# A decoder trunk on one core: the forget gates' product in four column groups, and the vectors' turn behind the modulation's last block

## The chip, the cores and the metric

One core of one Trainium2 chip runs the whole program in one launch. The time is device microseconds (us) of one execution. A kernel is run three times and more, and medians are compared. Engines are named as the profile names them: PE (TensorE, matrix multiply), PEld (its weight loads), DVE (VectorE), ACT (ScalarE), POOL (GpSimd), SP (SyncE, here only an issuer of DMAs).

## The reference, cut to what matters

Two layers of a causal decoder run over 1024 prompt tokens and 8 single-token samples (1032 columns, `NT`), model width 1024. In each layer a conditioning vector gives shifts, scales and gains (the modulation), a normed and modulated input `h` goes through one combined projection, and three mixers and a gated MLP follow. The part that the change touches is this:

```python
mod = jnp.dot(jax.nn.silu(c), ada_w) + ada_b                  # 1024 x 6144
sh1, sc1, g1, sh2, sc2, g2 = jnp.split(mod[:, None, :], 6, axis=-1)
h = rmsnorm(x, norms[0]) * (1 + sc1) + sh1
aq, ak, av, af, bq, bk, bv, bg, ca, cb = split_cols(jnp.dot(h, w_in))
logf = jax.nn.log_sigmoid((af + b_f).astype(F32))             # af: 4 columns of w_in
u = ca * jax.nn.sigmoid(cb)                                   # Conformer gate, then a conv of width 31
```

`af`, the forget gates' logits, has only 4 columns of `w_in` (one for each of 4 heads).

## The kernel before, in words

Activations lie with features on the 128 partitions and the 1032 tokens along the free axis; the model width is 8 slices `kk` of 128. The program is a chain of blocks with a barrier of all engines between them. In each block every engine has its own instruction list in the order of the code, and they meet through semaphores. For each layer the blocks are `block_modulation`, `block_project`, `block_mixer`, `block_tail`.

**Products.** `product3` makes one tile of 128 output rows in fp32r (a rounded float32 type) as three products: high weights by high input, high weights by low input, low weights by high input. Each is 3 matmuls of 260, 512 and 260 columns, so a slice `kk` is 9 matmuls and a tile 72. Weights come by DMA to `w_raw`; ACT rounds them to `w_hi`, POOL subtracts to get `w_lo`. Before a slice of the first tile, its hook `normed.on_pe` waits only until that slice of `h_hi` and `h_lo` is there.

**`block_modulation`.** Four blocks `b` of 512 modulation columns: PE multiplies the padded conditioning (32 stationary columns) in float32, on four column groups of the array, into `mp` (L333); ACT copies it to `mrow`; `turn(b)` turns it to partitions (L315); DVE adds the bias. `rows_of_vectors` turns the rows of biases, norms and conv weights (`vrow`) with four matmuls into `vp` (L322), and DVE copies these to `k.vecs` (L379) before anything in its list that uses them. DVE also sums squares (`macc`), PE sums them over partitions (`mst`, L405), and DVE makes the inverse root mean square from that in small operations, from a memset (L412) on. The instruction lists are strict: in DVE's, the copies of the vectors stand ahead of the additions of blocks 0 and 1, these ahead of the inverse root, and that ahead of blocks 2 and 3. The modulation's `ahead` loads the first two weight tiles of the projection and splits them, the forget tile at `COL_F` as one of them.

**`block_project`.** PE spreads the inverse root into `slot[0]` (L432). DVE, ACT and POOL then make `h` slice by slice. PE runs the forget tile first, a whole `product3` from the 128 columns at `COL_F`, of which only 4 are used, into `slot[1]`; its first instruction waits for slice 0 of `h`. Then it turns the conv contexts (L636), waits for ACT's copy of the 4 rows (`ft`, L706), turns these with 9 small matmuls (L643, `f_done`), and goes through the ten tiles of `tiles`. From the second of them on, every tile carries two slots of the remaining modulation (L651: 16 matmuls of 128 columns in float32, on four column groups, from `a_raw` in the memory of `k.x`) in front of slices 1 and 5. Before SP loads these it saves `k.x` to DRAM (`x_hold`) and waits for that. Each of the ten tiles waits for two counts:

```python
pe.wait_ge(lo_done, i + 2)
pe.wait_ge(free[s], i // 2 + s + 1)
```

The first two counts of `lo_done` are given by `pool.sem_inc` behind the last of POOL's operations on `h` (`normed.on_pool`), and the first count of `free[1]` by `act.sem_inc` behind the last of ACT's (`normed.on_act`). The forget tile waits for neither.

Of the kernel before, what the change touches and what calls it, by code (L numbers as in the profile page):

```python
# [22 lines left out]
P = 128  # L23
# [23 lines left out]
OFF = 252  # L47
# [6 lines left out]
for _name, _n in (("ident", 128), ("ones", 128), ("upto", 128), ("after", 128), ("mask", 128), ("pair", 128),  # L54
                  ("stack", 64), ("headsel", 2), ("sampsel", 8), ("decay", 512), ("xi", 256), ("zeta", 4), ("gchunk", 2),
                  ("gone", 2), ("pick", 9)):
    CONST[_name] = (_at, _n)
    _at += _n
# [3 lines left out]
def constants():  # L62
# [25 lines left out]
    put("pick", (r[:, None] % 32) == np.arange(9)[None, :])  # L88
    put("gone", np.exp(np.stack([log_g[2 * hh + hp] for hh in range(2)], 1)))
# [169 lines left out]
def block_modulation(k, L):  # L259
# [10 lines left out]
    with ExitStack() as ctx:  # L270
# [18 lines left out]
        ahead = Ahead(k, [w_in[:, :, COL_CA + DC:COL_CA + DC + P], w_in[:, :, COL_F:COL_F + P]])  # L289
# [19 lines left out]
        def _(pe):  # L309
# [212 lines left out]
def block_project(k, L):  # L522
# [4 lines left out]
    with ExitStack() as ctx:  # L527
# [5 lines left out]
        sig = ft = swap  # L533
# [27 lines left out]
        ring = lambda m: (m + 1) % 2  # L561
# [8 lines left out]
        def _(sp):  # L570
# [9 lines left out]
            for m, col in enumerate([COL_F] + tiles + [2 * HA * DA]):  # L580
                if m == 4:
# [6 lines left out]
                if 5 <= m < 5 + (PAIRS_LATE - 4) // 2:  # L588
                    for n in range(2 * m - 6, 2 * m - 4):
                        load_pair(n)  # L590
# [21 lines left out]
        def _(pool):  # L612
            plink = Link(pool, mod_link)
            plink(pool.memset(c_pad[:, :, :], 0.0))
# [4 lines left out]
            for m in range(2, 2 + nt):  # L619
# [7 lines left out]
        def _(pe):  # L627
# [3 lines left out]
            product3(pe, slot[1], k.w_hi[1], k.w_lo[1], k.h_hi, k.h_lo, KD, slice(0, P), normed.on_pe).then_inc(tile_done, 1)  # L631

            pe.wait_ge(side_loaded, 64)
            for half in range(2):
                for j in range(2):
                    last = pe.matmul(misc[1][:, 240 * j + 120 * half:240 * j + 120 * half + 120],  # L636
                                     crow[:, half, P * j:P * j + P], ident[0:120, 0:120], start=True, stop=True)
            last.then_inc(ctx_turned, 1)

            pe.wait_ge(free[1], 2)  # L640
            for c in range(TC):
                at = c * P if c < NC8 else NT - P
                last = pe.matmul(misc[0][:, HA * c:HA * c + HA], ft[0:HA, at:at + P], ident[0:HA, 0:HA], start=True, stop=True)  # L643
            last.then_inc(f_done, 1)
# [17 lines left out]
            def turn_tail():  # L662
                pe.wait_ge(free[1], 4)
# [31 lines left out]
        @block.scalar  # L695
        def _(act):
# [8 lines left out]
            act.wait_ge(tile_done, 1)  # L705
            act.activation(ft[0:HA, :], slot[1][0:HA, OFF:OFF + NT], ACT.Copy).then_inc(free[1], 1)  # L706
            for i in range(nt):
                if i + 2 < 2 + nt:
                    hi(i + 2)
                s = i % 2  # L710
# [9 lines left out]
                act.wait_ge(tile_done, i + 2)  # L720
                if i == 0:
                    act.wait_ge(f_done, 1)
                if i < 4:
                    if i == 2:
                        act.wait_ge(free[1], 3)
                    if i % 2 == 0:
                        act.activation(sig[:, :], res, ACT.Sigmoid).then_inc(free[0], 1)
# [7 lines left out]
                elif 4 <= i < 8:  # L735
                    j, dst = i % 2, (k.q_ret if i < 6 else k.k_ret)
                    scale = 1.0 if i < 6 else DB ** -0.5
# [3 lines left out]
                    else:  # L741
                        act.wait_ge(free[1], 4)
# [11 lines left out]
        def _(dve):  # L754
# [17 lines left out]
            for j in range(2):  # L772
                dve.wait_ge(free[0], 2 + j)
                dve.wait_ge(tile_done, 3 + 2 * j)
                dve.tensor_tensor(u[:, j, :], slot[1][:, OFF:OFF + NT], sig[:, :], ALU.mult).then_inc(free[1], 1)
                dve.wait_ge(free[1], 3 + j)
# [4 lines left out]
            for i in range(4, 8):  # L781
# [4 lines left out]
                dve.wait_ge(free[i % 2], {4: 4, 5: 5, 6: 5, 7: 6}[i])  # L786
# [1823 lines left out]
```

## Time and profile before

| | us |
|---|---|
| median of 3 runs (lowest, highest) | 2938.47 (2935.8, 2942.54) |
| the profiled execution, whole | 2943.78 |
| its span (first to last instruction) | 2941.5 |
| PE busy | 2808.8 (95%) |
| DVE busy | 1760.1 (60%) |
| ACT busy | 1190.2 (40%) |
| POOL busy | 199.9 (7%) |

A profile's busy time is a sum over stages with different limits. A timeline row gives the start, the length from the first start to the last end, the engine, line and operation, the number of records (x), and in brackets how long the engine sat idle before it and what ended that. A float32 matmul is two records, an fp32r matmul one. Times in the rows count from the start of the span. The first layer's modulation and projection lie at 27 to 234 us; the second layer's begin 1446 us later.

### The profile page before, as it was taken

The numbers are of one execution on the slowest core, as the hardware profiler recorded it, in microseconds if no ns is written. First come the engines' busy times: TensorE is split into PE (matmuls) and PEld (weight loads), VectorE is DVE, ScalarE is ACT, GpSimd is POOL, SyncE is SP. The second block draws the span as 40 slices with busy tenths as digits, with TensorE's granted clock in tenths as the row PEclk, the third lists the DMA queues.
The fourth block names the chain that finished last, engine by engine and source line by source line (L and its number), as shares of the span: only waits on it lengthen the run. The fifth ranks groups of instructions, "written<-read, shape, count | busy, mean of one in ns | idle before, by whom it ended". The sixth has DMA issues, their size and how long they took to land. (4 is left out here: it accounts for less than half of the span.)

```text
span 2941.5 us, 46421 instructions
## 1 busy us (share of the span) xinstructions
PE 2808.8 (95%) x18668; PEld 2463.5 (84%) x18668; DVE 1760.1 (60%) x2839; ACT 1190.2 (40%) x1897; POOL 199.9 (7%) x102
## 2 busy tenths in 40 slices
PE   6999999999999999999759999999999999999996
PEld 3888888778778899999738888897787888999995
DVE  4594444526776766676645743444567667666766
ACT  2241333525444444444332413345354445444442
POOL 1211110110000000000021210012000000000000
PEclk7999999999999999999869999999999999999998
DMA  5742112343333332333158311234332333323321
GB/s 218 234 130 51 52 51 73 93 139 94 93 94 93 93 94 88 94 93 94 32 183 244 89 48 51 52 86 122 120 96 86 94 99 93 96 87 94 94 87 69
DMA packets 430644, 293.56 MB, mean 100 GB/s; under 512 B 26493, under 2 KB 392613, under 8 KB 429630
## 3 DMA queue, kind: packets, MB, share of 16 engines
q1 hardware_dynamic: 426128, 288.45, 32.7%
q8 instruction: 148, 2.42, 0.3%
q10 hardware_dynamic: 4302, 2.15, 0.3%
q14 instruction: 66, 0.54, 0.1%
HBM read 267.68 MB, written 23.71 MB: 99 GB/s over the span
## 5 line engine op out<-in xcount | busy, mean ns | idle before, releaser
L1733 PE MATMUL tslot<-g_hi,w_hi 128*128 128x260 f32 (+1 forms) x2496 | 671.6, 323 | 9.8 <-DVE g_lo L2313 6.4
L1733 PE MATMUL tslot<-g_hi,w_lo 128*128 128x260 f32 (+1 forms) x2496 | 665.9, 321 | 0.0
L1733 PE MATMUL tslot<-g_lo,w_hi 128*128 128x260 f32 (+1 forms) x2496 | 663.5, 320 | 0.0
L1733 PEld LDWEIGHTS tslot<-g_hi,w_hi 128*128 128x128 f32 x2496 | 414.6, 189 | 52.6 <-issue 6.9
L1733 PEld LDWEIGHTS tslot<-g_hi,w_lo 128*128 128x128 f32 x2496 | 413.9, 189 | 38.0
L1733 PEld LDWEIGHTS tslot<-g_lo,w_hi 128*128 128x128 f32 x2496 | 414.0, 189 | 37.4
L1704 ACT ACTIVATE w_hi<-w_raw 128x1024 fp32r<-128x1024 f32 x292 | 307.1, 1052 | 331.5 <-PE tslot L2090 311.9
L1708 DVE TENSOR_TENSOR w_lo<-w_raw,w_hi 128x1024 fp32r<-128x1024 f32 x276 | 336.0, 1218 | 1.5 <-ACT w_hi L1704 1.5
L2398 DVE TENSOR_TENSOR cat<-cat,tslot 128x512 f32<-128x512 f32 (+1 forms) x320 | 220.5, 690 | 192.1 <-PE tslot L2090 190.9
L2090 PE MATMUL tslot<-f_hi,w_hi 128*128 128x260 f32 (+1 forms) x1056 | 283.2, 323 | 5.5 <-DVE w_lo L1708 3.3
L2090 PE MATMUL tslot<-f_hi,w_lo 128*128 128x260 f32 (+1 forms) x1056 | 281.8, 322 | 0.0
L2090 PE MATMUL tslot<-f_lo,w_hi 128*128 128x260 f32 (+1 forms) x1056 | 280.9, 320 | 0.0
L2361 DVE SCALAR_TENSOR_TENSOR bufs<-bufs,vecs 128x512 f32<-128x512 f32 x176 | 132.0, 750 | 229.3 <-ACT bufs L2238 229.3
L983 PE MATMUL dense<-h_hi,w_hi 128*128 128x344 f32 x672 | 228.9, 341 | 4.7 <-PEq L2554 4.7
L983 PE MATMUL dense<-h_lo,w_hi 128*128 128x344 f32 x672 | 217.2, 323 | 0.0
L983 PE MATMUL dense<-h_hi,w_lo 128*128 128x344 f32 x672 | 217.2, 323 | 0.0
L2090 PEld LDWEIGHTS tslot<-f_hi,w_hi 128*128 128x128 f32 x1056 | 175.2, 189 | 26.5 <-DVE cat L2398 5.5
L2090 PEld LDWEIGHTS tslot<-f_lo,w_hi 128*128 128x128 f32 x1056 | 175.7, 189 | 16.1
L2090 PEld LDWEIGHTS tslot<-f_hi,w_lo 128*128 128x128 f32 x1056 | 176.0, 190 | 14.7
L519 DVE SCALAR_TENSOR_TENSOR cat<-cat,vecs 128x1023 f32<-128x1023 f32 (+14 forms) x120 | 168.2, 1402 | 3.3
L2238 ACT ACTIVATE bufs<-bufs,vecs 128x520 f32<-128x520 f32 (+1 forms) x176 | 144.2, 820 | 18.3 <-ACT bufs L2230 0.4
L2230 ACT ACTIVATE bufs<-tslot 128x520 f32<-128x520 f32 (+1 forms) x176 | 105.5, 599 | 94.3 <-PE tslot L1733 91.4
(335 smaller groups left out, 3876.0 us busy)
## 6 DMA issues: line engine op xcount, KB each, us to landing
w_raw<-in_ffn_up_dram SPq DMA_DIRECT2D x176, 512.0 KB, 3.7
w_raw<-in_ffn_down_dram SPq DMA_DIRECT2D x88, 512.0 KB, 3.8
x_res<-in_ada_w_dram SPq DMA_DIRECT2D x64, 512.0 KB, 5.6
w_raw<-in_w_in_dram SPq DMA_DIRECT2D x46, 512.0 KB, 4.4
a_raw<-in_ada_w_dram SPq DMA_DIRECT2D x8, 2048.0 KB, 19.1
w_raw<-in_w_o_dram SPq DMA_DIRECT2D x32, 512.0 KB, 5.0
x_hold<-x_res SPq DMA_DIRECT2D x2, 4128.0 KB, 15.1
x_res<-x_hold SPq DMA_DIRECT2D x2, 4128.0 KB, 12.8
```

The lines of the kernel that those rows point to most:

```text
L519: return dve.scalar_tensor_tensor(acc, u[:, 0:TP - CTX + w], k.vecs[:, 1, 2 * w + j:2 * w + j + 1], acc, ALU.mult, ALU.add)
L983: last = pe.matmul(dense[p % 2][:, 0:b - a], w[:, kk, :], x[:, kk, a:b], start=(kk == 0 and first), stop=(kk == KD - 1 and w is w_lo))
L1704: act.activation(self.hi[n % 3][:, :, :], self.raw[n % 3][:, :, :], ACT.Copy).then_inc(self.hi_done, 1)
L1708: e.tensor_tensor(self.lo[n % 3][:, :, :], self.raw[n % 3][:, :, :], self.hi[n % 3][:, :, :].bitcast(F32), ALU.subtract).then_inc(self.dve ...
L1733: last = pe.matmul(out[:, at + a:at + b], w[:, kk, :], x[:, kk, t0 + a:t0 + b], start=(kk == 0 and first), stop=(kk == KD - 1 and w is w_lo))
L2090: last = pe.matmul(out[:, at + a:at + b], w, x[e][:, a:b], start=first and name == pairs[0], stop=final and name == pairs[-1])
L2230: act.activation(raw[half][:, 2:2 + w], out[:, at:at + w], ACT.Copy).then_inc(up_moved, 1)
L2238: act.activation(t_ab[half][:, 0:w], raw[half][:, 2:2 + w], ACT.Identity, scale=vec[:, 3, c:c + 1], bias=vec[:, 3, c + 2 * FT:c + 2 * FT + ...
L2361: dve.scalar_tensor_tensor(tt[:, 0:512], r[:, 1:513], tap1, tt[:, 0:512], ALU.mult, ALU.add).then_inc(conv, 1)
L2398: dve.tensor_tensor(y_m, y_m, out[:, at:at + w], ALU.add).then_inc(gathered, 1)
```

## The change

The forget gates no longer have a tile. Their 4 columns are loaded alone into a zeroed `wf_pad` of 32 columns, and after the first real tile PE multiplies them in plain float32 on four column groups (slices `kk` and `kk+4` on group `kk`), 48 matmuls into `slot[0]`. ACT copies all 128 rows to `ft` (now in `k.cat`), and the turn to tokens sums the four groups through a constant `pickf`. The tile list is one shorter; the two tiles loaded ahead are the first two real ones; slots and rings change parity. In the modulation, `rows_of_vectors` stands behind the product of block 3 in place of block 1.

```diff
-        ahead = Ahead(k, [w_in[:, :, COL_CA + DC:COL_CA + DC + P], w_in[:, :, COL_F:COL_F + P]])
+        ahead = Ahead(k, [w_in[:, :, COL_CA + DC:COL_CA + DC + P], w_in[:, :, COL_CA:COL_CA + P]])
...
-                if b == 1:
+                if b == 3:
                     rows_of_vectors()
                 if b >= 1:
                     turn(b - 1)
...
-            for m, col in enumerate([COL_F] + tiles + [2 * HA * DA]):
-                if m == 4:
+            for m, col in enumerate(tiles + [2 * HA * DA]):
+                if m == 0:
+                    sp.wait_ge(wf_zero, 1)
+                    sp.dma_start(wf_pad[:, :, 0:HA], w_in[:, :, COL_F:COL_F + HA]).then_inc(wf_loaded, 16)
+                if m == 3:
                     sp.dma_start(k.x_hold.rearrange("p (a b) -> p a b", b=NT), k.x[:, :, :]).then_inc(x_held, 16)
...
-            product3(pe, slot[1], k.w_hi[1], k.w_lo[1], k.h_hi, k.h_lo, KD, slice(0, P), normed.on_pe).then_inc(tile_done, 1)
...
+            def forget_product():
+                pe.wait_ge(wf_loaded, 16)
+                pe.wait_ge(free[0], 1)
+                for k0 in (0, 4):
+                    for x, first in ((k.h_hi, True), (k.h_lo, False)):
+                        for a, b in CHUNKS:
+                            for g in range(4):
+                                last = pe.matmul(slot[0][32 * g:32 * g + 32, OFF + a:OFF + b], wf_pad[:, k0 + g, :], x[:, k0 + g, a:b].bitcast(F32),
+                                                 start=(k0 == 0 and first), stop=(k0 == 4 and not first), skip_group_check=True)
+                last.then_inc(f_product, 1)
+
+            def forget_rows():
+                pe.wait_ge(free[0], 2)
+                for c in range(TC):
+                    at = c * P if c < NC8 else NT - P
+                    last = pe.matmul(misc[0][:, HA * c:HA * c + HA], ft[:, at:at + P], const(k, "pickf"), start=True, stop=True)
+                last.then_inc(f_done, 1)
...
+                    if i == 0:
+                        normed.on_pe(e, kk)
+                    if i == 1 and kk == 0:
+                        forget_rows()
                     if i >= 1 and kk in (1, 5):
                         mod_slot(2 * i - 2 + kk // 4)
...
             for i in range(nt):
-                s = i % 2
-                pe.wait_ge(lo_done, i + 2)
-                pe.wait_ge(free[s], i // 2 + s + 1)
-                product3(pe, slot[s], k.w_hi[s], k.w_lo[s], k.h_hi, k.h_lo, KD, slice(0, P), mod_hook(i)).then_inc(tile_done, 1)
+                s, w = slot_of(i), ring(i)
+                pe.wait_ge(lo_done, i + 1)
+                pe.wait_ge(free[s], i // 2 + (1 if s else 2))
+                product3(pe, slot[s], k.w_hi[w], k.w_lo[w], k.h_hi, k.h_lo, KD, slice(0, P), mod_hook(i)).then_inc(tile_done, 1)
+                if i == 0:
+                    forget_product()
+                    turn_contexts()
```

On PE, at the start of the first layer's projection, the order before is this. The three `pdiag` matmuls are the spread, and the first `h_hi,w_hi` is the forget tile; signal6 and signal7 count what DVE and POOL have made of `h`.

```order
L432 MATMUL slot<-pdiag,consts 128x260 [waits signal9]
L432 MATMUL slot<-pdiag,consts 128x512
L432 MATMUL slot<-pdiag,consts 128x260
L154 MATMUL slot<-h_hi,w_hi 128x260 [waits signal6,signal7]
L154 MATMUL slot<-h_hi,w_hi 128x512
```

At the same place of the changed kernel the first `h_hi,w_hi` is the tile at `COL_CA + DC`; signal24 is `free[1]` and signal26 is `lo_done`.

```order
L433 MATMUL slot<-pdiag,consts 128x260 [waits signal9]
L433 MATMUL slot<-pdiag,consts 128x512
L433 MATMUL slot<-pdiag,consts 128x260
L155 MATMUL slot<-h_hi,w_hi 128x260 [waits signal7,signal6,signal24,signal26]
L155 MATMUL slot<-h_hi,w_hi 128x512
```

The first product after the spread has two more waits. Behind that product PE's list before went on with the contexts, the 9 turns of the forget rows (`swap` is `ft`) and the first real tile.

```order
L154 MATMUL slot<-h_hi,w_lo 128x260
L636 MATMUL misc<-consts,ctxrow 128x120 [waits signal28]
L636 MATMUL misc<-consts,ctxrow 128x120 x3
L643 MATMUL misc<-consts,swap 128x4 [waits signal24]
L643 MATMUL misc<-consts,swap 128x4 x8
L154 MATMUL slot<-h_hi,w_hi 128x260 [waits signal23,signal26]
```

In the changed kernel the same stretch of PE's list reads so (`cat` is the new `ft`; signal23 is `free[0]`, signal43 `wf_loaded`).

```order
L155 MATMUL slot<-h_hi,w_lo 128x260
L655 MATMUL slot<-h_hi,wf_pad 32x260 [waits signal23,signal43]
L655 MATMUL slot<-h_hi,wf_pad 32x260 x3
L655 MATMUL slot<-h_hi,wf_pad 32x512 x4
L655 MATMUL slot<-h_hi,wf_pad 32x260 x4
L655 MATMUL slot<-h_lo,wf_pad 32x260 x4
...
L644 MATMUL misc<-consts,ctxrow 128x120 [waits signal28]
L644 MATMUL misc<-consts,ctxrow 128x120 x3
L663 MATMUL misc<-consts,cat 128x4 [waits signal23,signal26]
L663 MATMUL misc<-consts,cat 128x4 x8
L155 MATMUL slot<-h_hi,w_hi 128x260
```

The 48 matmuls stand between the first real tile and the contexts, and the forget rows are turned in front of the second real tile. In the modulation (first layer) PE's list in the changed kernel ends with the four turns of the vectors (`vp`) between the last product and the last two turns; before, they stood behind the second product.

```order
L334 MATMUL mp<-a_raw,c_pad 32x512 [waits signal3,a_early3]
L334 MATMUL mp<-a_raw,c_pad 32x512 x7
L323 MATMUL vp<-consts,vrow 128x88 [waits signal7]
L323 MATMUL vp<-consts,vrow 128x62
L323 MATMUL vp<-consts,vrow 128x88 x2
L316 MATMUL mtp<-consts,mrow 128x9 [waits signal5,signal3]
```

DVE's list is the same in both kernels, with the copies from `vp` ahead of all its additions and of the inverse root.

## Rows read from the trace of the kernel before

**Rows 1.** The page's part 1: busy time of PE, share of the span, instructions.
```profile
PE 2808.8 (95%) x18668; PEld 2463.5 (84%) x18668; DVE 1760.1 (60%) x2839; ACT 1190.2 (40%) x1897; POOL 199.9 (7%) x102
```

**Rows 2.** Timeline of PE, first layer's projection: start, length, row, [idle before <- releaser].
```profile
73.28 1.20 PE L154 MATMUL slot<-h_hi,w_hi 128*128 128x260 f32 x3 [6.94 <-POOL h_lo L468]
...
88.04 1.05 PE L636 MATMUL misc<-consts,ctxrow 120*128 120x120 f32 x8
...
91.42 1.23 PE L154 MATMUL slot<-h_hi,w_hi 128*128 128x260 f32 x3
...
104.32 0.63 PE L154 MATMUL slot<-h_hi,w_hi 128*128 128x260 f32 x3
...
105.83 1.08 PE L651 MATMUL misc<-x_res,pc_pad 128*32 128x128 f32 x32
106.84 0.74 PE L154 MATMUL slot<-h_hi,w_hi 128*128 128x260 f32 x3
```

**Rows 3.** Waits between 60 and 90 us: total, times, longest.
```profile
PE slot L154 <- POOL h_lo L468: 7.8, 3, 6.9
```

**Rows 4.** Timelines of POOL, ACT and SP in the same block.
```profile
82.65 2.42 POOL L468 TENSOR_TENSOR h_lo<-cat,h_hi 128x1024 fp32r<-128x1024 f32 x1 [1.28 <-ACT h_hi L481]
...
83.67 1.15 ACT L483 ACTIVATE h_hi<-cat,mod 128x1024 fp32r<-128x1024 f32 x1 [1.10 <-DVE cat L496]
...
82.65 1.02 SPq L593 DMA_DIRECT2D w_raw<-in_w_in_dram  x2
...
99.36 11.28 SPq L578 DMA_DIRECT2D x_res<-in_ada_w_dram  x8
```

**Rows 5.** Timelines of PE and ACT, second layer's projection.
```profile
1527.34 1.20 PE L154 MATMUL slot<-h_hi,w_hi 128*128 128x260 f32 x3 [6.94 <-POOL h_lo L468]
...
1537.73 1.15 ACT L483 ACTIVATE h_hi<-cat,mod 128x1024 fp32r<-128x1024 f32 x1 [1.10 <-DVE cat L496]
```

**Rows 6.** Windows: length, busy us (records) of each engine, PE clock, DMA.
```profile
28.20:33.30 5.10, 5.07 (x24) 1.19 (x28) 0.79 (x1) 2.84 (x3) 0.00 (x0) 0.50 1.05 407
33.30:36.00 2.70, 1.06 (x12) 0.12 (x4) 2.63 (x3) 2.70 (x4) 0.00 (x0) 1.00 1.07 395
...
91.30:94.40 3.10, 3.10 (x13) 2.81 (x13) 0.20 (x1) 1.28 (x1) 1.33 (x1) 0.50 1.13 490
```

**Rows 7.** Timeline of PE in the mixer: two float32 matmuls of 512 columns.
```profile
240.61 1.96 PE L996 MATMUL sc<-prob,consts 128*128 128x512 f32 x4
```

**Rows 8.** Timelines of PE, ACT and DVE, first layer's modulation.
```profile
41.12 2.43 PE L322 MATMUL vp<-consts,vrow 88*128 88x88 f32 x8 [6.76 <-DMA vrow<-in_ffn_conv_w_dram]
43.34 1.78 PE L315 MATMUL mtp<-consts,mrow 128*128 128x9 f32 x8
...
57.34 1.95 PE L315 MATMUL mtp<-consts,mrow 128*128 128x9 f32 x16
...
38.54 1.07 ACT L359 ACTIVATE mrow<-mp 128x512 f32<-128x512 f32 x2
...
43.66 0.69 DVE L379 COPY vecs<-vp 128x88 f32<-128x88 f32 x4 [2.32 <-PE vp L322]
...
54.11 0.07 DVE L412 MEMSET mv<- 128x9 f32 x1 [3.37 <-PE mst L405]
...
58.51 0.20 DVE L388 TENSOR_TENSOR mod<-mtp,vecs 128x36 f32<-128x36 f32 x1 [1.91 <-PE mtp L315]
...
59.56 0.23 DVE L398 SCALAR_TENSOR_TENSOR mod<-mod,vecs 128x72 f32<-128x72 f32 x1
```

**Rows 9.** Timelines of PE and DVE, second layer's modulation.
```profile
1492.87 2.37 PE L333 MATMUL mp<-a_raw,c_pad 128*32 128x512 f32 x16 [2.66 <-DMA a_raw<-in_ada_w_dram]
...
1499.11 3.64 PE L333 MATMUL mp<-a_raw,c_pad 128*32 128x512 f32 x16
...
1511.40 1.95 PE L315 MATMUL mtp<-consts,mrow 128*128 128x9 f32 x16
...
1513.63 0.23 DVE L398 SCALAR_TENSOR_TENSOR mod<-mod,vecs 128x72 f32<-128x72 f32 x1
```

More of the change, by code:

```diff
@@ L532, in block_project @@
         u = k.cat[:, 4:6, :]
-        sig = ft = swap
+        sig, ft = swap, k.cat[:, 2, :]
+        wf_pad = sb("wf_pad", [P, KD, 32])
         bf = sb("bf", [P, HA])
@@ L560, in block_project @@
         U_DONE = 3
-        ring = lambda m: (m + 1) % 2
+        ring = lambda m: m % 2
+        slot_of = lambda i: (i + 1) % 2
+        wf_zero, wf_loaded, f_product = (k.sem(n) for n in ("wf_zero", "wf_loaded", "f_product"))
         arena = k.x[:, :, :].rearrange("p a b -> p (a b)")
@@ L587, in _ @@
                         load_pair(n)
-                if 5 <= m < 5 + (PAIRS_LATE - 4) // 2:
-                    for n in range(2 * m - 6, 2 * m - 4):
+                if 4 <= m < 4 + (PAIRS_LATE - 4) // 2:
+                    for n in range(2 * m - 4, 2 * m - 2):
                         load_pair(n)
@@ L613, in _ @@
             plink = Link(pool, mod_link)
+            pool.memset(wf_pad[:, :, :], 0.0).then_inc(wf_zero, 1)
             plink(pool.memset(c_pad[:, :, :], 0.0))
@@ L618, in _ @@
             pool.sem_inc(lo_done, 1)
-            for m in range(2, 2 + nt):
+            for m in range(2, 1 + nt):
                 pool.wait_ge(hi_done, m - 1)
@@ L630, in _, with turn_contexts @@
             pe_spread(k, pe, diag, slot[0]).then_inc(rb_ready, 1)
-            product3(pe, slot[1], k.w_hi[1], k.w_lo[1], k.h_hi, k.h_lo, KD, slice(0, P), normed.on_pe).then_inc(tile_done, 1)
[L633 to L644, printed above, removed]
+            def turn_contexts():
+                pe.wait_ge(side_loaded, 64)
+                for half in range(2):
+                    for j in range(2):
+                        last = pe.matmul(misc[1][:, 240 * j + 120 * half:240 * j + 120 * half + 120],
+                                         crow[:, half, P * j:P * j + P], ident[0:120, 0:120], start=True, stop=True)
+                last.then_inc(ctx_turned, 1)
+            def forget_product():
[14 more added lines that the diff above has]
+                last.then_inc(f_done, 1)
             def mod_product(n):
@@ L662, in turn_tail @@
             def turn_tail():
-                pe.wait_ge(free[1], 4)
+                pe.wait_ge(free[0], 4)
                 for j in range(2):
@@ L703, in hi @@
                 act.activation(k.w_hi[ring(m)][:, :, :], k.w_raw[ring(m)][:, :, :], ACT.Copy).then_inc(hi_done, 1)
-            act.wait_ge(tile_done, 1)
-            act.activation(ft[0:HA, :], slot[1][0:HA, OFF:OFF + NT], ACT.Copy).then_inc(free[1], 1)
             for i in range(nt):
-                if i + 2 < 2 + nt:
-                    hi(i + 2)
-                s = i % 2
+                if i >= 1:
+                    hi(i + 1)
+                s = slot_of(i)
                 res = slot[s][:, OFF:OFF + NT]
@@ L719, in _ @@
                         act.activation(mrow[:, :], misc[1][:, 0:2 * P], ACT.Copy).then_inc(row_ready, 1)
-                act.wait_ge(tile_done, i + 2)
-                if i == 0:
-                    act.wait_ge(f_done, 1)
+                act.wait_ge(tile_done, i + 1)
                 if i < 4:
                     if i == 2:
-                        act.wait_ge(free[1], 3)
+                        act.wait_ge(free[0], 3)
                     if i % 2 == 0:
-                        act.activation(sig[:, :], res, ACT.Sigmoid).then_inc(free[0], 1)
+                        act.activation(sig[:, :], res, ACT.Sigmoid).then_inc(free[1], 1)
+                    if i == 0:
+                        act.wait_ge(f_product, 1)
+                        act.activation(ft[:, :], slot[0][:, OFF:OFF + NT], ACT.Copy).then_inc(free[0], 1)
                     if i == 3:
@@ L741, in _ @@
                     else:
-                        act.wait_ge(free[1], 4)
+                        act.wait_ge(free[0], 4)
                     for quad in range(4):
@@ L772, in _ @@
             for j in range(2):
[L773 to L776, printed above, removed]
+                dve.wait_ge(free[1], 2 + j)
+                dve.wait_ge(tile_done, 2 + 2 * j)
+                dve.tensor_tensor(u[:, j, :], slot[0][:, OFF:OFF + NT], sig[:, :], ALU.mult).then_inc(free[0], 1)
+                dve.wait_ge(free[0], 3 + j)
                 taps(*((0, 17) if j == 0 else (17, 26)))
@@ L785, in _ @@
                 dve.wait_ge(rope_raw, 3 * (i - 3))
-                dve.wait_ge(free[i % 2], {4: 4, 5: 5, 6: 5, 7: 6}[i])
+                dve.wait_ge(free[slot_of(i)], {4: 4, 5: 5, 6: 5, 7: 6}[i])
                 dve.tensor_tensor(swap[:, :], swap[:, :], rope[:, 1, :], ALU.mult).then_inc(rope_link, 1)
```

5 lines of the change are left out of this document (4 added, 1 removed).

## The prediction, as it was written before the result was known

> **What bounds the kernel now.** I read the page's busy times first: PE is busy for 95% of the span [rows 1], so an instruction taken from PE is worth its time wherever PE runs without a gap, and a gap on PE is worth its length. Next I read the timeline of PE in the first layer's projection [rows 2]. There PE is not dense at the front: it sits idle for 6.94 us until the first slice of `h` is split, starts the forget tile at 73.28 and ends it at 88.04. The waits of that stretch [rows 3] say that inside the tile only 7.8 - 6.94 = 0.86 us more are waited. The forget tile is therefore made almost wholly while DVE, ACT and POOL are still making `h`, which they end some 12 us after its start: the last operation of POOL on `h` starts at 82.65, that of ACT at 83.67 [rows 4]. From 88.04 on PE is dense. The second layer repeats it within 0.1 us [rows 5]. So the question is not only what the forget product costs, but what stands in its place under the making of `h`.
>
> **The start of the first tile.** In the changed order the first product of the block is a tile of the loop, and the loop waits for `lo_done` and `free[1]`, which the forget tile did not. Both counts are given behind the last piece of `h`, one by POOL, one by ACT. Slice-wise waits are still there, but they no longer matter, because the product cannot begin before all of `h` is nearly ready. When is such a count given? SP's weight loads wait for the same `lo_done`, and they are issued at 82.65, the very moment at which POOL's last operation starts [rows 4], not at its end, 85.07. So ACT's count comes at about 83.67 and the first tile starts then: 83.67 - 73.28 = 10.4 us later. If ACT's count comes only at the end of its operation (1.15 us), it is 11.5. What is got back is the 0.86 us of waits inside the tile. In the second layer it is 1537.73 - 1527.34 = 10.4 again [rows 5]. The half clock of a first tile, after PE's idle time, goes with it in either order. The end of the first tile moves by 10.4 - 0.9 = +9.5 us in each layer (up to +10.6).
>
> **The forget product.** It is 48 matmuls, that is 4 x 4 x 1032 = 16,512 columns, in float32 on four column groups. The trace has this kind twice. At full clock 16 matmuls of 128 columns take 106.84 - 105.83 = 1.01 us [rows 2], 0.493 ns a column, which gives 8.1 us. At half clock 24 records, 12 matmuls of 512 columns, take 5.1 us [rows 6], 0.83 ns a column or 0.415 at full clock, which gives 6.9 us. The chunks are 260 and 512 long, nearer to the second: I take 7.4 us. The clock at which it runs is full, I think: PE comes from a dense tile, and the window from 28.20 to 33.30 held just such products, and the one behind it ran at full clock [rows 6].
>
> Does the overlap of the groups hold? A full-width float32 matmul shows what four serial groups would cost: two matmuls of 512 columns in 1.96 us [rows 7], 1.91 ns a column, 3.9 times the first value. The rows therefore show nearly full overlap. The Trainium skill (TensorE: Matmul & The Clock Gate, Part 3: Packing small matmuls) is less generous: four tiles by rows measured 3.07x, three by columns 2.38x. By 3.07x the product would take 1.91 x 16,512 / 3.07 = 10.3 us in place of 7.4. The trace disagrees for 128 columns; for the chunk lengths here, only the changed kernel can say.
>
> **What goes.** One full tile per layer. The one from 91.42 to 104.32 took 12.9 us [rows 2], of which 3.1 us ran at half clock [rows 6], the fall that follows the small matmuls of contexts and forget rows. That fall stays, since the same small matmuls now stand ahead of the second real tile, so 12.9 - 1.55 = 11.35 us go. Contexts, copy and forget rows keep their 3.4 us (88.04 to 91.42): the copy is of 128 partitions in place of 4, with as many columns for each.
>
> Per layer: 9.5 + 7.4 - 11.35 = +5.55 us, and +11.1 for both (bounds +10.1 with 6.9 us, +14.7 with 8.1 and the late count). Behind it everything in the block moves with PE. SP loads one weight tile less ahead of its save of `k.x`, so the modulation's pairs come no later than now (first issue 99.36, in use at 105.83 without a gap), and PE asks for them at about 111: hidden. The load of `wf_pad`, its memset and the longer copy lie under 20 us in which PE waits for `h`. They cost nothing as long as that cover is there.
>
> **The modulation.** Before, in the first layer, PE sits idle 6.76 us at 41.12 until the vectors' rows land [rows 8]. Now turn 0 goes first. It needs ACT's first `mrow`, ready at 38.54 + 0.55, so it starts at about 39.15 in place of 43.34, 4.2 us earlier, and the last product, which ended when turns 2 and 3 began at 57.34, now ends at 57.3 - 4.2 = 53.1. Then come the vectors, 2.43 us at half clock or about 1.2 at full. Only then can DVE go on, and its list is strict: copies 0.69, two additions 0.4, the inverse root 54.11 to 58.51 - 1.91 = 56.60, that is 2.49, two more additions 0.4, the gain 0.23, with gaps 4.4 us in sum. Before, the inverse root lay under the last product; now it stands behind everything. The end comes at 53.1 + 2.43 + 0.1 + 4.4 = 60.0, or 58.8 with the fast turn, against 59.56 + 0.23 = 59.79: +0.2 to -1.0, say -0.3 us.
>
> In the second layer there is no such idle time to win. The vectors' rows are there early and PE waits for the big blocks instead: the second lands at 1492.87 [rows 9]. Product 1 ends at 1495.24, turn 0 at about 1496.95, and product 2 can start between then and 1499.11 (where it found its block landed before). I take the middle, 1.1 us earlier. The last product then ends at 1511.4 - 1.1 = 1510.3, and 2.43 (or 1.2) + 0.1 + 4.4 behind it is 1517.2 (1516.0), against 1513.63 + 0.23 = 1513.86: +2.7 us (bounds +1.1 and +4.4). Both layers: +2.4 us (+0.1 to +4.6).
>
> **Sum.** 11.1 + 2.4 = +13.5 us. The profiled execution took 2943.78 and would take 2957.3; it lies 5.3 us over the median of the runs, so I set the sum against that: 2938.47 + 13.5 = 2952.0 us, 2948.7 to 2957.8 by the bounds.
>
> **Rivals.**
> - *The first tile is not held back.* For it speaks that the counts could in principle be given early, being instructions of their own; against it, that the loads waiting for POOL's count are issued at 82.65 and no sooner. If so, tile 1 reaches its first modulation slot at 88.04 + 7.4 + 3.4 + 2.9 = 101.7, while the pair it needs is issued from 98.9 on (half of SP's 1.02 us less) and lands within 6.5 us (105.83 - 99.36), so of 4.1 us between 0.5 and 4.1 are won, say 2 per layer. With the modulation's +2.4: -1.6 us, 2936.9, no change. It decides for faster only if the pair lands within 3 us. 5%.
> - *The overlap of groups is that of the page's table*: 2.9 us more per layer, 2957.8. 8%.
> - *The product runs at half clock*: 14.8 us, +7.4 per layer, 2967. Against it, the windows of rows 6. 5%.
> - *The groups run one after the other*: 31.6 us, +24.2 per layer, 3001. Against it, rows 2 with rows 7. 1%.
> - *The modulation gains in both layers* (the vectors' turn and the inverse root cost nothing at the end): first layer -4, second -1, so 11.1 - 5 = +6, 2944.6. Against it, DVE's list, which is unchanged. 5%.
>
> **How the numbers follow.** The forecast has 76%. Its own range is 2948.7 to 2957.8; for 8 in 10 with the neighbours' share I take 2946 to 2959. A change within 0.2% (5.9 us) can't be told from none by this measurement. Faster by more than that: 2%, only if several terms fail at once. Within it: the first rival, and half of the last, 8%. Slower: 90%.
>
> **What would show it.** In the changed profile: (1) the first product of the projection starts at 83.5 to 85, not at 73.3, and PE's idle time before it is some 17 us; (2) its 48 small matmuls span 7 to 8 us at full clock; (3) the first modulation product of the projection starts near 111 in place of 105.83, with no wait for a DMA; (4) the first layer's modulation ends within 1 us of 59.8, the second's 2 to 4 us later relative to its start, with the inverse root behind the last product; (5) mixer and tail are unchanged in length. The prediction is wrong if the first tile starts before 80, or if the small matmuls take over 9 us.

## The result, and the profile after

The changed kernel takes 2948.85 us (median of 11 runs, 2942.89 to 2956.07); the kernel before, on the same chip, takes 2936.08 (11 runs, 2934.49 to 2942.93). The ratio is 1.0039, 95% interval 1.0027 to 1.0052, that is some 11.5 us slower (7.9 to 15.3). Forecast were +13.5 us and 2952.0.

The first rows are the page's busy times of the changed kernel's profiled execution, which took 2955.16 us with a span of 2953.2. They answer to [rows 1].

```profile
PE 2797.7 (95%) x18716; PEld 2446.7 (83%) x18716; DVE 1759.3 (60%) x2839; ACT 1188.0 (40%) x1895; POOL 195.6 (7%) x102
```

PE works 11.1 us less than before (2808.8) while the span is 11.7 us longer (2941.5 before). The work did go; what came is idle time of PE. Where it lies can be read in the timeline of PE in the first layer's projection, which answers to [rows 2] (start, length, row, [idle before <- releaser]):

```profile
60.71 3.81 PE L433 MATMUL slot<-pdiag,consts 128*128 128x260 f32 x6 [3.23 <-DVE pdiag L426]
81.91 1.20 PE L155 MATMUL slot<-h_hi,w_hi 128*128 128x260 f32 x3 [17.39 <-ACTq L725]
...
95.26 1.95 PE L655 MATMUL slot<-h_hi,wf_pad 128*32 128x260 f32 x24
97.03 1.92 PE L655 MATMUL slot<-h_lo,wf_pad 128*32 128x260 f32 x24
98.76 1.92 PE L655 MATMUL slot<-h_hi,wf_pad 128*32 128x260 f32 x24
100.50 1.92 PE L655 MATMUL slot<-h_lo,wf_pad 128*32 128x260 f32 x24
102.35 1.15 PE L644 MATMUL misc<-consts,ctxrow 120*128 120x120 f32 x8
103.66 2.14 PE L663 MATMUL misc<-consts,cat 128*128 128x4 f32 x18 [0.16 <-ACT cat L753]
105.66 0.72 PE L155 MATMUL slot<-h_hi,w_hi 128*128 128x260 f32 x3
...
107.80 1.93 PE L671 MATMUL misc<-x_res,pc_pad 128*32 128x128 f32 x32
```

Read it from the second row: the first tile begins after 17.39 us of idle time, released by ACT's queue, where it was 6.94 us and the first split slice of `h`. Then comes the forget product: its rows carry `wf_pad` and the shape 128*32, and it runs from 95.26 to 102.35. The 0.16 us ahead of the forget rows is ACT's copy, hardly waited for. No row ahead of L671 has a wait for a DMA.

Who released the first tile is seen beside it, in the timeline of ACT:

```profile
81.79 1.15 ACT L484 ACTIVATE h_hi<-cat,mod 128x1024 fp32r<-128x1024 f32 x1 [1.05 <-DVE cat L497]
```

and in that of SP, the DMA queues:

```profile
80.82 0.40 SPq L600 DMA_DIRECT2D w_raw<-in_w_in_dram  x1
81.26 0.58 SPq L589 DMA_DIRECT2D x_hold<-x_res  x1
95.43 11.84 SPq L582 DMA_DIRECT2D x_res<-in_ada_w_dram  x8
```

The tile starts 0.12 us after ACT's last operation on `h` *starts* (81.79), long before it ends (82.94). SP's weight load, which waits for POOL's count, goes at 80.82, the moment at which POOL's last operation on `h` starts:

```profile
80.82 2.40 POOL L469 TENSOR_TENSOR h_lo<-cat,h_hi 128x1024 fp32r<-128x1024 f32 x1 [1.34 <-ACT h_hi L482]
```

The windows of the forget product and of the first modulation product give their clock (the columns are those of [rows 6]):

```profile
95.26:102.35 7.09, 7.09 (x97) 3.06 (x96) 0.00 (x0) 1.05 (x1) 0.00 (x0) 1.00 0.88 239
107.80:109.66 1.86, 1.86 (x33) 1.36 (x33) 0.00 (x0) 0.00 (x0) 0.00 (x0) 0.50 1.02 292
```

The first ran at the upper level (1.00), the second at the lower (0.50): the fall of the clock behind the small matmuls is still there, as forecast. The second layer repeats the wait to the hundredth:

```profile
1541.91 1.20 PE L155 MATMUL slot<-h_hi,w_hi 128*128 128x260 f32 x3 [17.39 <-ACTq L725]
```

To compare many executions I cut each into stages, at instructions that every kernel has: *modulation* from the memset of `c_pad` to the start of DVE's `pdiag`, *projection* from there to the first dense matmul of the mixer, then the rest. All in us, first layer / second layer; "rest" is what lies between the projection and the next layer, or the end. The 26 to 28 us ahead of the first `c_pad` are in no column.

| kernel | modulation | projection | rest | span |
|---|---|---|---|---|
| before | 33.45 / 41.53 | 173.51 / 173.62 | 1239.01 / 1252.71 | 2941.5 |
| before, again | 30.47 / 41.51 | 173.64 / 173.61 | 1236.05 / 1252.77 | 2936.1 |
| changed | 32.76 / 40.77 | 178.28 / 178.71 | 1240.95 / 1255.19 | 2953.2 |
| changed, again | 31.62 / 41.48 | 178.43 / 178.40 | 1237.63 / 1254.87 | 2949.8 |

The projection stage repeats within about 0.3 us in these two kernels, and it is 4.8 to 5.1 us longer per layer in the changed one: 9.6 to 9.9 us of the whole. The first layer's other stages differ between two executions of one kernel by as much as between the kernels. The second layer's rest does not: it repeats within 0.4 us in each kernel and is 2.1 to 2.5 us longer in the changed one. Most of that lies in the mixer (from the end of the projection to DVE's memset of `bufs`): 332.31 and 331.97 us against 330.24 and 330.26. Its last 7 us, first in the changed kernel, then in the one before, show a spell of the lower clock in the one and none in the other:

```profile
2023.32:2030.32 7.00, 4.21 (x20) 3.62 (x18) 0.29 (x2) 1.08 (x2) 0.00 (x0) 0.65 0.00 0
2012.03:2019.03 7.00, 4.21 (x36) 3.78 (x34) 0.58 (x2) 1.07 (x2) 0.00 (x0) 1.00 0.00 0
```

Of the kernels in the experiments below that have the forget product, e3, e5 and e7 are long there too (331.5 to 332.0) and e1 and e6 are not (329.1 and 330.3), so the product alone does not set it; what does is not shown.

### The profile page after: what moved, and what is told of

It reads as the page before. It is cut to its first block and busy times, and to the rows that moved or that the text cites. A ratio compares the mean times of both kernels' runs of the same rounds, so it can differ in the third digit from the quotient of the medians.

```text
span 2953.2 us, 46513 instructions
## 1 busy us (share of the span) xinstructions
PE 2797.7 (95%) x18716; PEld 2446.7 (83%) x18716; DVE 1759.3 (60%) x2839; ACT 1188.0 (40%) x1895; POOL 195.6 (7%) x102
```

## The experiments

Two theories were to be told apart, and a third was tried beside them. **The held-back tile:** the first product is now a tile of the loop, which waits for the end of the making of `h`; this costs some 9.5 us per layer, and the forget product on four column groups is a gain in itself. **The product:** the small matmuls (or the clock they leave behind) cost more than the tile that they replace. And **the vectors:** their move costs something at the end of the modulation.

### e1_first_tile_free: the changed kernel without the wait

```
-                pe.wait_ge(lo_done, i + 1)
-                pe.wait_ge(free[s], i // 2 + (1 if s else 2))
+                if i >= 1:
+                    pe.wait_ge(lo_done, i + 1)
+                    pe.wait_ge(free[s], i // 2 + (1 if s else 2))
```

> The changed kernel, whose first tile of the projection no longer waits for lo_done and free[1] (only slice by slice for h, as the forget tile did). My theory, that these two waits cost 9.5 us per layer: the first tile starts 6.9 us after the spread's end in place of 17.4, the forget product follows some 15 us later, and PE then reaches its first modulation product about 101 on the old time axis, where it waits 1 to 3 us for its pair, since the save of k.x has not moved. In sum 6 to 9 us per layer less than the changed kernel: 2931 to 2937, at or a little under the kernel before. Rival, that the loss lies in the forget product, in its copy of 128 rows or in the clock: under 4 us are won, 2945 to 2949.

2937.99 us, ratio to before 0.9991 (0.9978 to 1.0005): the loss is gone. Projection 173.68 / 171.83. The waits of PE between 58 and 240 us:

```profile
PE slot L155 <- POOL h_lo L469: 7.9, 3, 6.9
PE misc L671 <- DMA x_res<-in_ada_w_dram: 4.2, 1, 4.2
```

The first row is that of [rows 3] again (7.8, 3, 6.9). The second is new: with the tile early, the modulation's product is what waits, longer than the 1 to 3 us expected. The projections are 4.6 and 6.9 us shorter than in the changed kernel's first profile, where 6 to 9 had been expected. The timeline of PE shows where the wait is:

```profile
96.72 0.63 PE L155 MATMUL slot<-h_hi,w_lo 128*128 128x260 f32 x3
101.59 1.69 PE L671 MATMUL misc<-x_res,pc_pad 128*32 128x128 f32 x32 [4.23 <-DMA x_res<-in_ada_w_dram]
```

and that of SP why:

```profile
80.23 0.58 SPq L589 DMA_DIRECT2D x_hold<-x_res  x1
95.69 12.18 SPq L582 DMA_DIRECT2D x_res<-in_ada_w_dram  x8
```

The save of `k.x` is issued at 80.23 and the pairs that overwrite it only at 95.69, behind the save's landing; the first of them is wanted at 97.35. So the time that the early tile frees on PE is partly spent waiting for this transfer. This is the first rival of the prediction made real: of the 4.1 us per layer that it had to win, none is won in the first layer (4.23 us waited) and 1.8 us in the second (1.60 us waited).

### e2_gate_in_before and e9_gate_again: the kernel before with the wait

```
             pe_spread(k, pe, diag, slot[0]).then_inc(rb_ready, 1)
+            pe.wait_ge(lo_done, 1)
+            pe.wait_ge(free[1], 1)
             product3(pe, slot[1], k.w_hi[1], k.w_lo[1], k.h_hi, k.h_lo, KD, slice(0, P), normed.on_pe).then_inc(tile_done, 1)
```

> The kernel before, with the two waits (lo_done at 1, free[1] at 1) put ahead of its forget tile, nothing else. My theory: +9.5 us per layer, 2955 (ratio 1.0065), with the first tile at 83.7 in place of 73.3. Rival, that such a wait is free because the product would stand still for the slices of h anyway, or that a later wait absorbs it: under +3 us in all, 2936 to 2939.

> The kernel before with the two waits ahead of its forget tile, once more. In its first profile the two projections were 8.0 and 8.8 us longer than before, 16.8 in sum, but the whole 26.8; the other 10 us lay in stages whose code is that of before. If they were half-clock spells that this execution happened to get, this profile shows projections of 181.5 and 182.4 again and other lengths elsewhere, with a median nearer to +17. If they belong to the kernel (its later stages always begin at a moment at which the clock falls), the median is +27 again and the long stages are the same ones.

2968.61 us, ratio 1.0091 (1.0068 to 1.0114); again, on another chip, 2962.72 us, 1.0080 (1.0050 to 1.0110). The timeline of PE in the first of them shows the same wait as the changed kernel:

```profile
86.30 1.20 PE L154 MATMUL slot<-h_hi,w_hi 128*128 128x260 f32 x3 [17.39 <-ACTq L700]
```

The projection is 181.50 / 182.43 and 182.48 / 182.50: +8.0 to +9.0 us per layer over before. So the wait alone costs 17 to 18 us in the two projections (19 had been expected), more than the whole loss of the changed kernel, and the forget product gives a part back: the changed kernel's projections are 3.2 to 4.2 us shorter than these, where 11.35 - 7.4 = 3.95 had been worked out. By their ratios the two runs of this kernel lose another 6 to 10 us, more than expected and outside the stage that the edit touches; the part on the clock takes that up.

### e3_vectors_back: the changed kernel with the vectors where they were

```
-                if b == 3:
+                if b == 1:
                     rows_of_vectors()
```

> The changed kernel with the turn of the vectors back behind the modulation's product 1. By the prediction's sum the move cost 2.4 us, so this is 2946.5. By the trace of the changed kernel, where both modulations were 0.7 us shorter than before, the move won 1.4 us and this is 2950. The stage lengths (from the memset of c_pad to the first pdiag) say it more sharply than the time: 32.9 and 41.5 us by either view if the turn stands where it stood.

### e4_vectors_alone: the kernel before with only the vectors moved

```
-                if b == 1:
+                if b == 3:
                     rows_of_vectors()
```

> The kernel before with the turn of the vectors moved behind product 3, nothing else. By the prediction's sum +2.4 us, 2938.5; by the stage lengths of the changed kernel's trace -1.4 us, 2934.7. If the second layer's modulation was short there only because PE held the full clock, its length here depends on the clock: 40.8 us with full clock over turns and sums, 44 us at half.

e3: 2949.7 us, 1.0031 (1.0017 to 1.0045), like the changed kernel. e4: 2939.85 us, 0.9996 (0.9981 to 1.0011), like the one before. In the table the modulation of all kernels, by place of the vectors, us:

| vectors behind | first layer | second layer |
|---|---|---|
| product 1 (before twice, gate twice, e3) | 33.45, 30.47, 37.47, 35.07, 33.59 | 41.53, 41.51, 41.94, 35.74, 37.83 |
| product 3 (changed twice, e1, e4, e5) | 32.76, 31.62, 31.61, 33.21, 29.95 | 40.77, 41.48, 40.99, 41.40, 42.43 |
| product 2 (e6) | 30.35 | 41.33 |

Within one place the stage spreads by 1.7 to 7 us. Much of that is the granted clock, as the whole stage of the second layer shows in before, e3 and the changed kernel (the clock is the number ahead of the last two):

```profile
1473.64:1515.17 41.53, 24.13 (x122) 13.01 (x122) 12.89 (x31) 12.23 (x14) 4.71 (x3) 0.58 0.64 232
1476.17:1514.00 37.83, 20.24 (x122) 10.68 (x122) 12.88 (x31) 12.23 (x14) 4.71 (x3) 0.64 0.69 254
1478.53:1519.30 40.77, 20.11 (x122) 9.63 (x122) 12.66 (x32) 12.24 (x14) 4.70 (x3) 0.67 0.64 236
```

At a mean clock of 0.58 the stage takes 41.0 to 41.5 us in either place. In the executions that got a higher one it is shorter with the turn behind product 1 (37.83 at 0.64; 35.74 at 0.69 in e9) than behind product 3 (40.77 at 0.67). So a cost of some 3 us, as forecast for this layer, may be there in one clock and hidden in the other; three profiles don't settle it. The term of +2.4 us for both layers is neither seen nor excluded, and e4's interval (-5.6 to +3.2 us) says the same.

### e5_free_and_early_save: e1 with the save one weight tile earlier

```
-                if m == 3:
+                if m == 2:
                     sp.dma_start(k.x_hold.rearrange("p (a b) -> p a b", b=NT), k.x[:, :, :]).then_inc(x_held, 16)
+                if m == 3:
                     sp.wait_ge(x_held, 16)
```

> The changed kernel with the first tile free of lo_done and free[1], and with the save of k.x issued right behind the side loads, some 20 us earlier (k.x is not written in between). With the first tile free PE stood 4.2 us (first layer) and 1.6 us (second) for the modulation's first pair, whose load waits for that save. My theory: with the save out of the way these waits are gone, each projection is a tile less and a forget product more, 11.35 - 7.1 = 4.2 us under the 173.5 us of before, 169.3 us; the whole 5 to 10 us under the kernel before (ratio 0.997). Rival, that the pairs come late for another reason (the 8 MB behind them, or h_scaled), or that the earlier save disturbs the making of h: projections of 172 us and more.

2936.52 us, 0.9987 (0.9975 to 0.9999). The projection is 169.34 / 167.84. The timeline of SP:

```profile
79.57 0.40 SPq L601 DMA_DIRECT2D w_raw<-in_w_in_dram  x1
80.66 12.87 SPq L582 DMA_DIRECT2D x_res<-in_ada_w_dram  x8
```

and of PE:

```profile
97.43 1.06 PE L155 MATMUL slot<-h_hi,w_lo 128*128 128x260 f32 x3
98.43 1.22 PE L672 MATMUL misc<-x_res,pc_pad 128*32 128x128 f32 x32
```

The pairs leave 15 us earlier, and the product that waited 4.23 us follows without a gap. Against the kernel before the projection is now 4.2 / 5.8 us shorter, against the changed kernel 8.9 / 10.9 us. The 4.2 us are what the forget product on four column groups is worth once nothing waits (11.35 - 7.09 = 4.26); the second layer's other 1.5 us are the clock. Behind the small matmuls it did not fall there, and in e6, whose projection is built the same, it did (169.35 us). The stretch from the forget rows to the first modulation product, in e5 and in e6:

```profile
1549.89:1551.48 1.59, 1.59 (x12) 1.25 (x11) 0.20 (x1) 0.00 (x0) 1.25 (x1) 1.00 1.06 244
1545.03:1547.88 2.85, 2.85 (x10) 2.23 (x10) 0.20 (x1) 0.00 (x0) 1.13 (x1) 0.50 0.87 238
```

Of the 10 us won in the two projections the ratio shows only 3.8 (0.3 to 7.4), less than the 5 to 10 expected. In this profile the first tail took 912.4 us, which the part on the clock takes up.

### e6_free_save_vectors_2: e5 with the vectors behind product 2

```
-                if b == 3:
+                if b == 2:
                     rows_of_vectors()
```

> The kernel of the run before this one in the list (first tile free, early save), with the vectors turned behind product 2 in place of 3. In the first layer their rows have landed by then, and copies and inverse root lie under product 3 again: the first modulation 31.4 us (33.4 before, 31.6 to 33.2 with the turn behind product 3). In the second 42.5 us at half clock, as in the kernel before or 1 us over. Rival, that the differences between such modulations are only the clock that each execution happens to get: 31 to 37 and 38 to 43 us in any order.

2935.32 us (12 runs, 2925.56 to 2945.24), 0.9968 (0.9952 to 0.9983). Projection 169.36 / 169.35. Its interval (5.0 to 14.1 us under the kernel before) is the only one that lies well below 1; those of e5 and e7 end at 0.9999. That product 2 is a better place than product 3 is not shown by it: its modulation (30.35 / 41.33) is inside the spread above, and the medians of e5, e6 and e7 lie within 2.2 us.

### e7_free_save_root_first: e5 with the inverse root ahead of the copies on DVE

```
+            dve.wait_ge(sums_ready, 1)
+            dve_inverse_rms(k, dve, link, st, v, t)
             dve.wait_ge(rows_turned, 1)
...
-                if b == 2:
-                    dve.wait_ge(sums_ready, 1)
-                    dve_inverse_rms(k, dve, link, st, v, t)
```

> First tile free, early save, vectors behind product 3, and in DVE's list the inverse root moved ahead of the copies of the vectors, where it needs only the sums. If the inverse root is what ends the modulation (my prediction's tail of 4.4 us), each modulation is 2.0 to 2.5 us shorter than with the same order and the root behind. Rival, from the trace of the changed kernel: PE's turns 2 and 3 also wait for the first addition and end only 0.3 us before or behind the root, so that moving the root wins 0 to 0.5 us.

2937.46 us, 0.9984 (0.9969 to 0.9999): nothing over e5. Its modulation is 32.90 / 42.80 against 29.95 / 42.43 there, where 2.0 to 2.5 us less had been expected if the root were the end of the stage. In the second layer DVE's timeline shows the root done by 1506.0 and the end no sooner for it:

```profile
1505.82 0.17 DVE L166 SCALAR_TENSOR_TENSOR inv<-mt,inv 128x9 f32<-128x9 f32 x1
1508.65 0.69 DVE L382 COPY vecs<-vp 128x88 f32<-128x88 f32 x4 [2.66 <-PE vp L323]
1509.38 0.29 DVE L388 TENSOR_TENSOR mod<-mtp,vecs 128x36 f32<-128x36 f32 x2
1511.60 0.20 DVE L388 TENSOR_TENSOR mod<-mtp,vecs 128x36 f32<-128x36 f32 x1 [1.93 <-PE mtp L316]
1513.31 0.20 DVE L388 TENSOR_TENSOR mod<-mtp,vecs 128x36 f32<-128x36 f32 x1 [1.51 <-PE mtp L316]
```

DVE now waits 1.93 and 1.51 us for PE's last two turns. Those turns wait in their own place for DVE's first additions, so moving the root only changes who waits.

### e8_changed_again and e10_before_again: the two kernels once more

No edit; the runs show what repeats.

> The changed kernel once more, on the same chip as these three, for a second profile and a ratio from the same runs of the kernel before. Projection stages 178.3 and 178.7 us again to within 0.3 if the two waits set them; modulations 32 to 33 and 41 to 44 us; ratio 1.003 to 1.005.

> The kernel before, for a second profile. Projections 173.5 us again to within 0.3. The modulations 32 to 37 and 38 to 42 us, the tails 905.5, 908.5, 910.5 or 912.5 us, by how often the clock falls in them: if so, a single profile's whole length says nothing finer than 10 us about this change, and stage lengths do.

Changed: 2949.21 us, 1.0023 (1.0012 to 1.0034), where 1.003 to 1.005 had been expected; before, a single execution: 2938.28. Their stages stand in the table above. The two intervals for the changed kernel, 7.9 to 15.3 us and 3.5 to 10.0 us, overlap between 8 and 10, where the projections' 9.6 to 9.9 lie.

## The clock spells behind

Why do whole times stray by 5 us when the projection repeats within 0.3? The tail of a layer (from DVE's memset of `bufs`, L2335, to the next layer's memset of `c_pad`; in the second layer to PE's first matmul into `ybank`) is the same code in all kernels. The changed kernel, windows of its first tail and of two stretches in it:

```profile
568.29:1478.50 910.21, 882.14 (x5482) 784.15 (x5482) 592.82 (x922) 399.70 (x646) 20.33 (x8) 0.98 0.31 95
590.29:598.29 8.00, 8.00 (x29) 6.64 (x29) 0.00 (x0) 1.06 (x1) 2.04 (x1) 0.57 0.92 281
670.29:678.29 8.00, 6.01 (x37) 6.01 (x38) 6.17 (x18) 2.52 (x4) 0.00 (x0) 0.79 0.44 132
```

The same stretches in the second run of the same kernel:

```profile
569.25:1475.05 905.80, 877.60 (x5482) 780.53 (x5482) 595.02 (x923) 399.63 (x646) 20.13 (x8) 0.99 0.31 96
591.25:599.25 8.00, 8.00 (x43) 6.75 (x43) 0.00 (x0) 1.63 (x3) 1.05 (x1) 1.00 0.95 289
671.25:679.25 8.00, 8.00 (x62) 7.42 (x62) 5.73 (x18) 2.50 (x5) 0.00 (x0) 1.00 0.45 131
```

PE has 5482 matmul records in both, but in the first the granted clock is low some 23 us and again some 104 us behind the tail's start, and 4.4 us are lost. By the means of the two windows (0.57 and 0.79, between 0.50 and 1.00) these spells last about 7 and 3.4 us. Over all profiles the tail took about 905.5, 908.7, 910.2 or 912.4 us and hardly anything between. In the profile of e9 (gate in the kernel before) both took 912.4, 14 us more than the two tails of before's second profile, which is more than what this execution loses outside its projections. In that of e2 one did, 7 us; the rest of its loss lies in the first layer's modulation (37.47 us) and mixer (332.87). But the first tails of e5 and e7 and the second of e6 took 912.4 too, with no such wait. Whether the wait makes the long tails likelier, or they merely fell so, is open: two profiles of that kernel don't settle it.

One regularity stands in the twelve profiles: behind each of the nine mixers that were longer than 331.5 us, whose last 7 us ran at a mean clock of 0.64 or 0.65, the tail took 905.6 to 905.8 us. Behind the fifteen others it took 908.5 to 912.4 us eleven times and 905.3 to 905.5 four times. So such spells are not independent of each other, and what an edit does to one stage can return in a later one. No run here shows why.

## Why the prediction was right, point by point

- **The start of the first tile** was the deciding step, and it held: forecast 10.4 us later with ACT's count at the start of its operation, measured from `pdiag` 22.61 in place of 12.16, which is 10.45, in both layers. The other bound (11.5, the count at the end) is out. e1 and e2 show from both sides that this wait is the cause: taken out, the loss goes; put into the kernel before, it costs 8.0 to 9.0 us of projection per layer, without any small matmul. The end of the tile moved by 9.04 and 9.39 us, forecast 9.5. So 1.41 and 1.06 us came back inside the tile, where the working had the 0.86 us of the waits' brackets. PE's rows in the kernel before show that a wait costs more than its bracket:

```profile
80.53 0.63 PE L154 MATMUL slot<-h_hi,w_lo 128*128 128x260 f32 x3
81.42 0.74 PE L154 MATMUL slot<-h_hi,w_hi 128*128 128x260 f32 x3 [0.26 <-POOL h_lo L468]
82.00 0.64 PE L154 MATMUL slot<-h_lo,w_hi 128*128 128x260 f32 x3
```

  Undisturbed rows of this kind start 0.47 us apart; here it is 0.89 and 0.58, so 0.53 us went with a wait of 0.26. Both waits together cost 1.4 us in either layer. The half-clock part at the front was 0.1 us shorter than before in the first layer and 0.3 us longer in the second.
- **The forget product**: forecast 7.4 us (6.9 to 8.1) at full clock, measured 7.09 at granted clock 1.00, and 7.08 to 7.09 in both layers of every kernel that has it. The size of chunks was the right thing to go by: 7.09 us for 16,512 columns is 0.43 ns a column, near the 0.415 from 512 columns and below the 0.493 from 128. Against the serial 1.91 of [rows 7], which is one row of two matmuls, that is an overlap of 4.4. The table of the Trainium skill (TensorE: Matmul & The Clock Gate, Part 3: Packing small matmuls) has 3.07x for four tiles by rows; an estimate by that factor is 10.3 us. This trace does not agree (7.09), and the measurement decides.
- **The tile that goes** was put at 11.35 us. What is left of the measured +4.77 and +5.09 after the two steps above is 4.77 - 9.04 - 7.09 = -11.4 and 5.09 - 9.39 - 7.09 = -11.4. That is a remainder, not a reading: it holds whatever else changed in the stage. Contexts, copy and rows take 105.66 - 102.35 = 3.3 us, forecast 3.4.
- **The sum per layer**: forecast +5.55, measured +4.8 to +5.1; both +9.6 to +9.9 for +11.1. The forecast was too high by the 0.3 us of the product and the 0.1 to 0.5 of the tile's end.
- **The pairs' load is hidden**: right, the first modulation product starts 48.50 us behind `pdiag` in place of 44.71, with no wait. That is 3.8 us later where 5.2 had been worked out, by the smaller terms above and because part of the half clock now lies behind this start: the product itself takes 1.86 us at 0.50, and took 1.01 at full clock. e1, where it starts without the first tile's wait, shows the next bound: 4.23 us waited.
- **The modulation**: the weak step. The order on DVE was foreseen (copies, additions, root, additions, gain), and the tail from the copies' start to the gain's end takes 57.97 - 53.54 = 4.4 us, as worked out. But e7 shows that the root is not what makes the tail: PE's turns 2 and 3 end as late. The timeline of PE in the changed kernel has the link that I had left out:

```profile
52.01 1.42 PE L323 MATMUL vp<-consts,vrow 88*128 88x88 f32 x8
54.60 2.87 PE L316 MATMUL mtp<-consts,mrow 128*128 128x9 f32 x16 [1.17 <-DVE mod L389]
```

  and that of DVE its end:

```profile
53.54 0.69 DVE L380 COPY vecs<-vp 128x88 f32<-128x88 f32 x4 [13.33 <-PE vp L323]
54.26 0.30 DVE L389 TENSOR_TENSOR mod<-mtp,vecs 128x36 f32<-128x36 f32 x2
...
57.51 0.19 DVE L389 TENSOR_TENSOR mod<-mtp,vecs 128x36 f32<-128x36 f32 x1 [0.27 <-PE mtp L316]
57.74 0.23 DVE L399 SCALAR_TENSOR_TENSOR mod<-mod,vecs 128x72 f32<-128x72 f32 x1
```

  The two turns wait for the first additions, which wait for the vectors' copies, so they stand in the tail as well and DVE waits 0.27 us for them. And the second layer's stage did not grow: 40.77 and 41.48 against 41.53 and 41.51, where +2.7 was forecast (+1.1 to +4.4). The working priced this stage at the clock that [rows 9] had (0.58 on average). Where both places were seen at a higher one, e3 at 0.64 and the changed kernel at 0.67, the turn behind product 3 is 2.9 us longer, as forecast; at 0.58 it is not. What the move is worth over many executions stays open.
- **The signs**: the first tile starts at 81.91 and not at 83.5 to 85, and the first modulation product at 107.80 and not near 111, partly because the first modulation began 1.1 us sooner in this execution and was 0.7 us shorter. Counted from `pdiag` the first sign holds. The first layer's modulation ended within 1 us of the forecast, counted from its start; the second's did not come later. Mixer and tail were not unchanged in length, as the second mixer's 1.7 to 2.1 us show.
- **The rivals**: the serial product, the half clock and the overlap of 3.07 are all out by the 7.09 us at clock 1.00. A modulation that gains 5 us in both layers is out as well: with the vectors put back (e3) the changed kernel is no slower (1.0031 against 1.0039 and 1.0023). The free first tile is e1, and its working held in kind: of the 4.1 us per layer to win, -0.2 and 1.8 were won, 1.6 together where 4 had been taken, since the pair was late. The whole was put at 1.6 us under before; the ratio 0.9991 says 2.6 under (6.5 under to 1.5 over).
- **The whole time** came out 3.2 us below the forecast and inside the range; 2.4 of these are that the kernel before was itself at 2936.08 in these runs, not at the 2938.47 that the sum was set against. That closeness is partly luck: the +2.4 us of the modulation are not seen, the projections gave 1.2 to 1.5 us less than forecast, and the second layer's rest gave 2.1 to 2.5 us that no step of the working had. What bears the forecast out is the projection stage.

## What to carry to other kernels

When a product that could start on the first slice is replaced by one from a loop, read what the loop waits for: a tile that is spread under the making of its input is nearly free, and the work that takes its place at the front inherits the wait, not the freedom. When a wait on the bounding engine goes, look at the transfers that its length had covered, and move them by as much (e5). And where whole times stray by clock spells, compare the one stage that the edit touches between two marks that both kernels have; 4.8 us in 178 could be read there to a few tenths. Look at the clock inside that stage too: a spell more or less was 1.5 us between e5 and e6. And look at the stages that the edit does not touch, since one of them moved by 2 us here.

## What the hardware did that I had not expected

- A count given by an instruction of its own behind an operation in the queue of ACT or POOL comes when that operation *starts*: PE starts at 81.91 with ACT's last operation on `h` at 81.79 to 82.94. For POOL it is SP's issue at 80.82, and 82.65 in [rows 4]. It is harmless here, since the product waits per slice as well, but such a count doesn't say that the data is there.
- Four column groups of float32 were 4.4 times as fast as the full-width matmuls of [rows 7] (7.09 us; 31.5 by 1.91 ns a column), with chunks of 512 and 260 columns, even with a load of weights ahead of every matmul record (96 loads in the window, 3.06 us busy).
- The same 5482 matmul records of the first tail take 905.5, 908.7, 910.2 or 912.4 us, in steps. In the two executions of the changed kernel, the 4.4 us between them go with two spells of about 7 and 3.4 us at the lower clock, present in the one and absent in the other.
